# The order of the expert weight loads: each expert's down weights ahead of the gate-up weights of the second next expert

## The reference

```
def expert_step(acc, params):
    wgu, bgu, wd, bd, g = params
    hgu = xt @ wgu + bgu                                   # wgu: 1024 x 2048
    gate = jnp.minimum(hgu[:, :D_EXPERT], SWIGLU_LIMIT)
    up = jnp.clip(hgu[:, D_EXPERT:], -SWIGLU_LIMIT, SWIGLU_LIMIT)
    y = ((up + 1.0) * (gate * jax.nn.sigmoid(SWIGLU_ALPHA * gate))) @ wd + bd   # wd: 1024 x 1024
    return acc + g[:, None].astype(y.dtype) * y, None
acc, _ = lax.scan(expert_step, zeros, (w_gate_up, b_gate_up, w_down, b_down, gates.T))
out = rmsnorm(h + acc, norm_final_g)
```

## Time and profile before

| | us |
|---|---|
| median of 3 runs | 1177.08 (1175.77 to 1180.67) |
| the profiled execution's own time | 1176.43 |
| its span, first to last instruction | 1174.9 |
| PE busy | 1080.4 (92% of the span) |
| DVE, ACT, POOL busy | 204.2, 152.9, 27.8 |
| share of the expert loads' queue (q1) | 88.8% of 16 DMA engines' span |
| granted TensorE clock, mean | 0.993 |

### The profile page before, as it was taken

The page is one execution under the profiler, slowest core; times in us unless marked ns, Lnnn a source line. Parts: engine busy times, 40 slices in busy tenths (PEclk is TensorE's granted clock), DMA queues, the critical chain, the costliest instruction groups (busy, mean ns, idle before and its releaser), DMA issues.

```text
span 1174.9 us, 15024 instructions
## 1 busy us (share of the span) xinstructions
PE 1080.4 (92%) x6238; PEld 483.5 (41%) x6238; DVE 204.2 (17%) x434; ACT 152.9 (13%) x327; POOL 27.8 (2%) x71
## 2 busy tenths in 40 slices
PE   8999999989999988888888888888888888888896
PEld 6677888543333333333333333333333333333322
DVE  2312213123111111111111111111111111111112
ACT  1154222230000000000000000000000000000002
POOL 0010000210000000000000000000000000000000
PEclk9999999989999999999999999999999999999998
DMA  9961527389999999999999999999999999999991
GB/s 323 335 253 72 214 91 279 136 329 419 428 427 428 428 427 428 428 428 428 428 428 428 430 428 428 429 428 429 429 428 428 428 428 428 428 428 428 428 385 53
DMA packets 44456, 437.18 MB, mean 372 GB/s; under 512 B 5336, under 2 KB 6416, under 8 KB 19632
## 3 DMA queue, kind: packets, MB, share of 16 engines
q1 hardware_dynamic: 42256, 435.19, 88.8%
q10 hardware_dynamic: 2176, 1.65, 0.6%
HBM read 435.76 MB, written 1.06 MB: 372 GB/s over the span
## 4 chain that ended last, share of the span: by engine, by line
DMA 57%; PE 41%; DVE 1%; ACT 0%; issue 0%; SPq 0%; POOL 0%; DVEq 0%; POOLq 0%
DMA ring<-in_w_down_dram 56%; PE bank L1299 12%; PE bank L1055 9%; PE bank L1271 7%; PE bank L1153 2%; PE bank L1165 2%; PE bank L1058 2%; PE bank L1251 1%; DMA ring<-in_w_in_dram 1%; PE bank L1242 1%; PE bank L1123 0%; PE bank L1290 0%; PE bank L1098 0%; PE bank L1353 0%; PE bank L1188 0%
## 5 line engine op out<-in xcount | busy, mean ns | idle before, releaser
L1271 PE MATMUL bank<-ring,gates 128*64 128x512 f32 x2048 | 466.5, 598 | 0.0
L1299 PE MATMUL bank<-ring,gates 128*64 128x512 f32 x1024 | 232.3, 597 | 75.3 <-DMA ring<-in_w_down_dram 75.3
L1271 PEld LDWEIGHTS bank<-ring,gates 128*64 128x64 f32 x2048 | 139.3, 137 | 238.1 <-issue 227.5
L1299 PEld LDWEIGHTS bank<-ring,gates 128*64 128x64 f32 x1024 | 68.8, 136 | 237.2 <-DMA ring<-in_w_down_dram 121.1
L927 DVE TENSOR_SCALAR gates<-bank 128x512 f32<-128x512 f32 x32 | 22.1, 692 | 759.5 <-PE bank L1271 759.5
L1055 PE MATMUL bank<-ring 128*128 128x256 f32 x384 | 85.0, 381 | 0.0
L1055 PEld LDWEIGHTS bank<-ring 128*128 128x128 f32 x384 | 72.3, 190 | 11.3 <-issue 1.3
L1251 PE MATMUL bank<-gates,scatter_w 64*128 64x512 f32 x256 | 63.6, 615 | 0.7 <-ACT gates L675 0.7
L671 ACT ACTIVATE gates<-gates 128x512 f32<-128x512 f32 x32 | 20.1, 629 | 275.4 <-DVE gates L927 275.4
L1242 PEld LDWEIGHTS bank<-onehot,qkT 128*128 128x128 bf16 x1488 | 45.1, 98 | 25.1 <-issue 25.1
L675 ACT ACTIVATE gates<-bank 128x512 f32<-128x512 f32 x32 | 19.1, 597 | 264.1 <-PE bank L1299 264.1
(11 more groups left out here) (181 smaller groups left out, 518.6 us busy)
## 6 DMA issues: line engine op xcount, KB each, us to landing
ring<-in_w_gate_up_dram SPq DMA_DIRECT2D x128, 2048.0 KB, 26.0
ring<-in_w_down_dram SPq DMA_DIRECT2D x63, 2048.0 KB, 25.5
ring<-in_w_in_dram SPq DMA_DIRECT2D x9, 2048.0 KB, 21.4
ring<-in_w_out_dram SPq DMA_DIRECT2D x1, 4096.0 KB, 12.7
ring<-in_w_in_dram SPq DMA_DIRECT2D x4, 512.0 KB, 8.4
ring<-in_w_proj_sb_dram SPq DMA_DIRECT2D x1, 2048.0 KB, 9.2
ring<-in_w_proj_moba_dram SPq DMA_DIRECT2D x1, 2048.0 KB, 7.4
ring<-in_w_down_dram SPq DMA_DIRECT2D x2, 1024.0 KB, 17.0
```

Of the source, the lines that this page charges most:

```text
L1271: ins = mm(bank[4 + i][SLOTS * c:SLOTS * (c + 1), :], xeT[:, k, :], ring[:, base + k // 2, n0:n0 + CH], start=False, stop=k == KD - 1)
L1299: ins = mm(bank[6][SLOTS * c:SLOTS * (c + 1), :], rows, ring[:, place, j * D + c * CH:j * D + (c + 1) * CH], start=k == 0, stop=k == KD - 1)
```

## The change

In `experts` of SP each down load is issued ahead of the four gate-up loads behind which it used to stand. Where the order was gu2; gu3, dn1; gu4, dn2; ... gu31, dn29, dn30, dn31, it is now gu2; dn1, gu3; dn2, gu4; ... dn29, gu31, dn30, dn31. The loads are the same, with the same slots and the same waits; PE, DVE, ACT and POOL have the same instructions in the same order.

```
             def experts(done):
                 load_gate_up(2, 0, done)
                 with sp.Fori(0, E // 2 - 2) as i:
+                    load_down(i * 2 + 1, done)
                     load_gate_up(i * 2 + 3, GU, done)
-                    load_down(i * 2 + 1, done)
+                    load_down(i * 2 + 2, done)
                     load_gate_up(i * 2 + 4, 0, done)
-                    load_down(i * 2 + 2, done)
+                load_down(E - 3, done)
                 load_gate_up(E - 1, GU, done)
-                load_down(E - 3, done)
                 load_down(E - 2, done)
                 last_down(done)
```

## The result

| | before | changed |
|---|---|---|
| median of 20 runs, us | 1179.31 | 1181.38 |
| lowest | 1175.49 | 1178.31 |
| profiled execution, us | 1176.43 | 1182.24 |
| its span | 1174.9 | 1180.7 |

Two of the twenty runs before (1829.09 and 1248.93) were slow ones and count in no comparison. The ratio is 1.0021 with a 95% interval of 1.0012 to 1.0029: 2.5 us slower, 1.4 to 3.4. The forecast was no change within 0.5%, at +1.4 us.

What follows compares the result with a forecast made beforehand. From about 370 us the stream of weights at 428 GB/s bounds the kernel. A 16.0 us delay goes into the 18 us by which the stream ended early, leaving +1.4: span 1176.3, plus 1.5, 1177.8 us; range 1175 to 1182.

Steps and rivals of the forecast that it cites:

- The start: After gu2 the stream stands idle until dn1 s0 is issued at 286.7; it falls behind by 16.0 us.
- dn30's row: Load near the end, before the change: dn30 s1 landed 6.6 us after dn30 s0, so 1.7 us lost behind a restart.
- The middle: Laps of the loop: nothing changes; PE's 3.4 us of waits move to other slots, the lap stays 29.36 us.
- The rival of the longer queue: In the laps, more queued loads slow the stream; a lap 1% longer gives 1185.4 us; chance 0.08.
- The end: Last experts: gu31's 19.6 us of loads come after dn29, so less work remains behind the last bytes; PE ends 1.4 later.
- The rival that the loss isn't paid back: At the program's end, PE's turn behind dn29 keeps its length, so the whole 16.0 comes out: 1192.4 us; chance 0.04.
- the faster rival: At the start, dn1 is issued without delay or the stream catches up; the 16.0 vanishes: near 1163 us; chance 0.04.
- The level: Whole run: the forecast built on the profiled execution, 1176.43 us; the median before, 1177.08, lay 0.65 above it.
- a second thin restart: Allowance in the range's high end: a further 1.7 us lost if the stream restarts on a thin queue again.

Runs made afterwards that it cites:

- experiment 6: New order of loads from dn5 to dn28 only, gu31 again ahead of dn29, against the kernel before: 1180.97 us, ratio 1.0025.
- Experiment 1: Changed kernel with gu31 issued ahead of dn29 again, the new order kept in the loop: 1196.64 us, ratio 1.0146 against before.
- experiment 2: Kernel before with only dn29 moved ahead of gu31, old order in the whole loop: 1175.04 us, ratio 0.9957.
- experiment 3: Kernel before with the new order of loads from dn5 on, to the end: 1165.82 us, ratio 0.9884.
- experiment 5: Kernel before with the old order up to dn2 and the new one from dn3 on: 1171.22 us, ratio 0.9948.

## Why the prediction was right, point by point

PE reached the first down product 3.3 us later in the profile of the changed kernel than in that of before, so each forecast time is shown with 3.3 added.

| step | forecast | with 3.3 | measured |
|---|---|---|---|
| dn1 s0 issued | 286.7 | 290.0 | 290.0 |
| from issue to landing on an idle queue | 7.7 | | 7.9 |
| dn5 s1 landed | 417.5 | 420.8 | 421.5 |
| lap | 29.36 | | 29.365 |
| waits in a lap | 2 on L1299, 1 on L1271 | | 1.94 and 0.80 |
| dn29 s1 landed | 1122.2 | 1125.5 | 1126.3 |
| last load landed | 1161.4 | 1164.7 | 1165.4 |
| last down product | 1158.2 | 1161.5 | 1162.3 |
| against before | +1.4 | | +2.5 (1.4 to 3.4) |

**The start.** The idle stretch is where it was put. The mis-sized term is the loss behind it: I let the new order lose the 0.8 us that the old one loses over twelve slots; it lost 1.3 us within seven slots of the restart, and 0.2 in the first landing. That is 0.7 us more, a delay of 16.7 and not 16.0, and it stands in every later row of the table (421.5 against 420.8). It isn't the loss of dn30's row either, where the very next load came 1.7 us late: here dn1 s1 landed 4.8 behind dn1 s0 and gu3 s0 5.0 behind that, and the lateness came with gu3 s1, in a stream that moved 426 GB/s or more. What causes it stays open.

**The middle.** Nothing, as experiment 6 shows. Four gate-up loads were issued in 1.9 to 2.6 us each time, and took up to 43.4 us to land, nine slots' worth, so SP was not held; and the slices show 427 to 431 GB/s, so the stream did not slow down. The rival of the longer queue falls. The waits sum to 71.7 us where I said 75 to 80: there are three in a lap now, 2.74 us together, where PE's slack is 3.4. The rest is probably in the reading: a group of matmuls is shown as 3.65 us long and the next begins 3.5 after its start, so each wait reads some 0.2 us short.

**The end.** Experiment 1 shows that the return is real and sits where it was put. The rival that the loss isn't paid back comes true in that kernel, at 1196.6. The time of the faster rival, "near 1163", doesn't follow from its own terms: 1177.8 - 16.0 is 1161.8.

**The level.** 1177.8 was forecast for 1181.4. Of these 3.6 us, 2.9 come from taking the profiled execution of before (1176.43) for a typical one, when the median of twenty runs is 1179.31; it was an execution without the half-clock stretch at 262. I had put this at 0.65, from three runs. The other 0.7 is that of the start. That 1181.38 lies within the stated 1175 to 1182 is partly luck: the range had 0.8 us at its top for the level, and what made room for the rest was 1.7 us for a second thin restart that didn't come. The slice near 280 fell to 30% and not to half in part for the same reason: 3.3 us more of idle stream are 11% of a slice; the rest is that the slices begin a little later here and that the stream stood still before gu2 s3 counted as landed (108 GB/s from 270 to 275).

**What the forecast missed is a better kernel.** The sum had a loss of 16 us and a return of nearly as much, and I didn't ask if they could be had apart. They can: the loss depends on where the order changes, the return only on the order of the last loads. Changing at dn5 keeps the return and loses 2.6 us: that kernel is 1.2% faster than before, and 1.4% faster than the changed kernel (0.9884 against 1.0021).

## What to carry to other kernels

Where one stream of loads bounds a loop, as here, its order inside the loop moves waits about without changing the lap. So read the two ends: how long the queue runs dry when the order first makes the issuer wait, and how much compute stands behind the last bytes. A load that waits for its buffer should have enough queued ahead of it to cover the time until that buffer comes free; switch to the order of use only once such a backlog exists. And compare profiles from an event that both programs reach alike, the latest one ahead of the change if you can (down 28 in experiment 2), since a clock stretch ahead of it can be larger than the effect.

## What the runs showed of the hardware

After the 20.27 us wait of experiment 1, TensorE ran its next matmuls at half clock; the granted clock was 0.50 during the wait (1130 to 1140). The windows of that kernel across the end of the wait:

```profile
1140.00:1145.00 5.00, 4.58 (x14) 1.43 (x16) 0.00 (x0) 0.00 (x0) 0.00 (x0) 0.61 0.62 262
1145.00:1150.00 5.00, 5.00 (x28) 1.72 (x26) 0.00 (x0) 0.60 (x1) 0.00 (x0) 1.00 0.66 206
```

Through the laps, with waits of 0.7 to 1.7 us, the granted clock is 1.00 (421 to 1126, before and changed). The stretch between 262 and 278 is less plain: there PE had been busy without a gap since 245, at full clock from 250 to 262, and fell to 1.2 GHz in eight of ten profiles and not in the other two (before, and experiment 6). What decides it stays open; it made PE 3.3 us later in the profile of the changed kernel.

A load of 2 MB issued when the queue was idle, or had at most one load left, took 7.5 to 9.1 us from issue to landing (7.7 and 7.9 above, 7.6 in experiment 2, 7.5 in experiment 3, and 9.1 at dn3 in experiment 5). In an unbroken stream a load lands every 4.89 us. The load behind the first one landed 4.8 to 6.6 us after it.
